# Down projections as seven block products in a hybrid encoder's FFN, on one Trainium2 core

## What is computed

```
for l in range(2):
  h = x + 0.5 * swiglu(rmsnorm(x, ffn1_norm), wg, wu, wd)
  p = rmsnorm(h) @ w_in ; retention heads and differential attention heads
  h = h + concat(ret, dif) @ w_out
  h = h + 0.5 * swiglu(rmsnorm(h, ffn2_norm), wg, wu, wd)
  x = rmsnorm(h, final_norm)
swiglu(x) = (silu(x @ wg) * (x @ wu)) @ wd
```

## Time and profile before

| | us |
|---|---|
| median of 3 runs (lowest, highest) | 1898.19 (1897.99, 1898.59) |
| the profiled execution | 1898.53 |
| its span | 1896.70 |
| PE busy | 1879.3 |
| POOL busy | 1206.0 |
| DVE busy | 1143.2 |
| ACT busy | 910.6 |

### The profile page before, as it was taken

One profiled execution on the slowest core, in us unless ns is written; L12 is line 12 of the kernel. 1 busy time (PEld: TensorE's weight loads), 2 busy tenths in 40 slices (PEclk: granted clock), 3 DMA queues, 4 the chain that ended last, 5 costly groups with the idle time before them and its releaser, 6 DMA issues.

```text
span 1896.7 us, 29712 instructions
## 1 busy us (share of the span) xinstructions
PE 1879.3 (99%) x11518; PEld 1673.4 (88%) x11518; DVE 1143.2 (60%) x1865; ACT 910.6 (48%) x1505; POOL 1206.0 (64%) x814
## 2 busy tenths in 40 slices
PE   9999999999999999999999999999999999999997
PEld 7989989878888989989889898998778889899896
DVE  7727657438756745727676476663587477366273
ACT  7525445456425534524565254445564365255252
POOL 6867767555435767857468576765554377678582
PEclk9999999999999999999999999999999999999999
DMA  4333323232223232332224223223222133324231
GB/s 157 137 99 125 134 84 112 78 100 67 67 67 111 90 112 90 106 97 105 83 101 157 73 106 112 89 90 111 78 67 78 46 111 112 111 90 134 67 110 69
DMA packets 54999, 186.46 MB, mean 98 GB/s; under 512 B 6440, under 2 KB 7976, under 8 KB 54860
## 3 DMA queue, kind: packets, MB, share of 16 engines
q1 hardware_dynamic: 53136, 181.61, 28.7%
q10 hardware_dynamic: 1724, 2.96, 0.5%
HBM read 182.44 MB, written 3.15 MB: 98 GB/s over the span
## 4 chain that ended last, share of the span: by engine, by line
PE 88%; POOL 6%; DVE 2%; ACT 2%; issue 1%; DMA 0%; SPq 0%; DVEq 0%; ACTq 0%; POOLq 0%
PE bank L693 17%; PE bank L695 17%; PE bank L694 17%; PE pair L693 9%; PE pair L695 9%; PE pair L694 9%; POOL w_lo L596 2%; PE pair L988 1%; POOL w_lo_x L615 1%; POOL w_lo L615 1%; PE pair L1012 1%; PE bank L973 1%; PE bank L1024 1%; PE bank L731 1%; PE bank L740 1%
## 5 line engine op out<-in xcount | busy, mean ns | idle before, releaser
L587 POOL TENSOR_TENSOR w_lo<-raw,w_hi 128x512 fp32r<-128x512 f32 (+1 forms) x240 | 314.8, 1336 | 382.5 <-ACT w_hi L1091 382.2
L693 PE MATMUL bank<-hg_hi,w_hi 128*128 128x256 f32 (+1 forms) x1396 | 447.1, 320 | 0.7 <-DVE bank L1581 0.7
L694 PE MATMUL bank<-hg_lo,w_hi 128*128 128x256 f32 (+1 forms) x1396 | 441.4, 316 | 0.0
L695 PE MATMUL bank<-hg_hi,w_lo 128*128 128x256 f32 (+1 forms) x1396 | 441.2, 316 | 0.0
L693 PEld LDWEIGHTS bank<-hg_hi,w_hi 128*128 128x128 f32 x1396 | 264.8, 190 | 22.1 <-issue 3.9
L694 PEld LDWEIGHTS bank<-hg_lo,w_hi 128*128 128x128 f32 x1396 | 265.0, 190 | 18.2 <-issue 1.2
L695 PEld LDWEIGHTS bank<-hg_hi,w_lo 128*128 128x128 f32 x1396 | 265.1, 190 | 17.6
L1091 ACT ACTIVATE w_hi<-raw 128x1024 fp32r<-128x1024 f32 (+1 forms) x120 | 124.2, 1035 | 262.2 <-PE bank L695 124.6
L1548 DVE SCALAR_TENSOR_TENSOR h<-pair,h 128x512 f32<-128x512 f32 x100 | 68.9, 690 | 258.6 <-PE pair L695 258.5
L693 PE MATMUL pair<-a_hi,w_hi 128*128 128x512 f32 x440 | 172.7, 393 | 1.9 <-issue 1.3
L695 PE MATMUL pair<-a_hi,w_lo 128*128 128x512 f32 x440 | 171.7, 390 | 0.0
(11 more groups left out here) (292 smaller groups left out, 4904.0 us busy)
## 6 DMA issues: line engine op xcount, KB each, us to landing
raw<-in_w_gu SPq DMA_DIRECT2D x96, 512.0 KB, 3.7
raw_x<-in_w_gu SPq DMA_DIRECT2D x80, 512.0 KB, 4.1
raw<-in_w_p SPq DMA_DIRECT2D x56, 512.0 KB, 3.5
raw_x<-in_w_dn SPq DMA_DIRECT2D x32, 512.0 KB, 3.8
raw<-in_w_dn SPq DMA_DIRECT2D x32, 512.0 KB, 3.6
raw<-in_w_o SPq DMA_DIRECT2D x16, 512.0 KB, 3.4
raw_x<-in_w_dn SPq DMA_DIRECT2D x16, 384.0 KB, 3.4
raw<-in_w_dn SPq DMA_DIRECT2D x16, 384.0 KB, 3.5
```

Source lines behind the costliest of these rows:

```text
L587: ins = pool.tensor_tensor(columns(lo_[:, part, :]), source[:, part.start * P:part.stop * P], columns(hi[:, part, :]).bitcast(F32), ALU.su ...
L693: pe.matmul(out, hi[:, 0, :], m_hi, start=first, stop=False)
L694: pe.matmul(out, hi[:, 0, :], m_lo, start=False, stop=False)
L695: return pe.matmul(out, lo_[:, 0, :], m_hi, start=False, stop=last)
```

## The change

The down projections of the first two chunks (PAIRED = 2) become blocks of the same kind as fast tiles. A block takes two output tiles (2q, 2q + 1) by even and odd gated tiles, tokens halved, so four blocks of 84 matmuls take the place of eight units. Blocks and tiles form one list of 28 per FFN, and all engines walk it in one order. The third chunk keeps its plain units. What a block needs of the activations is made for each pair of gated tiles: S1 to S4, sums and differences of token halves of the even and the odd tile.

```diff
+BLOCKS = []
+for _c in range(len(CHUNKS)):
+    BLOCKS += [("t", _c, _i) for _i in range(0 if _c else CLASSIC, CHUNKS[_c])]
+    if _c < PAIRED:
+        BLOCKS += [("d", _c, _q) for _q in range(KD // 2)]
...
+            def lo_s2(l, f, c, j):
+                n = mixture_index(f, c, j)
+                pool.wait_ge(s2_hi, at(s2_hi, l, n + 1))
+                pool.tensor_tensor(s2_l[:, j, :], even[:, 0:SEQ], s2_h[:, j, :].bitcast(F32), ALU.subtract)\
+                    .then_inc(s2_lo, 1)
```

POOL's queue in an FFN, after the classic units and the opening of the first two blocks, both as before:

```diff
+                for b in range(NB):
+                    kind, c, i = BLOCKS[b - 1] if b else ("", 0, 0)
+                    if kind == "t" and c < PAIRED and i % 2:
+                        lo_s2(l, f, c, i // 2)
+                    if b + 1 < NB:
+                        lo_differences(l, f, b + 1)
+                        lo_b22(l, f, b + 1)
+                    if b == 0:
+                        lo_s2(l, f, 0, 0)
+                    if b + 2 < NB:
+                        lo_gate(l, f, b + 2)
+                        differences(l, f, b + 2)
+                    elif b + 2 == NB:
+                        lo(l, down_unit(f, 0))
```

ACT's queue in the slot of block b (c and i are those of the block before it):

```diff
+                if kind == "t":
+                    silu(l, f, c, i)
+                copy_p1(l, f, b)
+                if not first_pair(b):
+                    hi_t4(l, f, b)
+                if paired and i % 2 == 0:
+                    copy_even(l, f, c, i)
+                if kind == "t":
+                    hi_gated(l, f, c, i)
+                if first_pair(b):
+                    hi_t4(l, f, b)
+                if paired and i % 2:
+                    hi_s14(l, f, c, i // 2)
+                    hi_s2(l, f, c, i // 2)
+                if b + 1 < NB:
+                    copy_t1(l, f, b + 1)
+                    hi_differences(l, f, b + 1)
+                    hi_t2(l, f, b + 1)
+                    hi_b22(l, f, b + 1)
```

DVE, with waits left out; for c < PAIRED fast_mult ends in gated_product, without the second product with the norm. FUNCTIONS_AT is {0: 1, 2: 2, 4: 3}. ACT makes its exponentials of part 0 before step 0 and those of part 2 after step 3's silu:

```diff
             def classic_up(l, f, i):
-                dve.tensor_tensor(up[:, :], gate_up[i][1], norm(f), ALU.mult).then_inc(up_ready, 1)
+                dve.tensor_copy(up[:, :], gate_up[i][1]).then_inc(up_ready, 1)
...
+            def gated_product(l, f, c, i):
+                if i % 2:
+                    dve.tensor_tensor(gated, gated, up[:, :], ALU.mult).then_inc(act_ready, 1)
+                    return
+                dve.tensor_tensor(gated[:, 0:SEQ], gated[:, 0:SEQ], up[:, 0:SEQ], ALU.mult)
+                dve.tensor_tensor(even[:, SEQ:T], gated[:, SEQ:T], up[:, SEQ:T], ALU.mult).then_inc(act_ready, 1)
+            def token_difference(l, f, c, i):
+                dve.tensor_tensor(gated[:, SEQ:T], gated[:, 0:SEQ], even[:, SEQ:T], ALU.subtract).then_inc(s3_done, 1)
+            def gated_mixtures(l, f, c, i):
...
+                dve.tensor_tensor(even[:, 0:SEQ], even[:, 0:SEQ], gated[:, SEQ:T], ALU.subtract).then_inc(s2_done, 1)
+                dve.tensor_tensor(s14[:, 0:SEQ], gated[:, SEQ:T], even[:, SEQ:T], ALU.add).then_inc(s1_done, 1)
+                dve.tensor_tensor(s14[:, SEQ:T], gated[:, 0:SEQ], even[:, 0:SEQ], ALU.add).then_inc(s4_done, 1)
+            def pair_outputs(l, f, b):
...
+                for out in (gated, odd_out):
+                    dve.scalar_tensor_tensor(out=out, in0=out, scalar=0.5, in1=norm(f), op0=ALU.mult, op1=ALU.mult)
+                for k, out in ((2 * q, gated), (2 * q + 1, odd_out)):
+                    dve.tensor_tensor(h[:, k, :], out, h[:, k, :], ALU.add).then_inc(h_ready, 1)
+            def former_output(l, f, b):
+                if l and f == 0 and 2 <= b < 2 + KD:
+                    scale_h(l - 1, b - 2)
...
             def attention(l):
+                layer_functions(l, 0)
                 dve.wait_ge(rms_ready, at(rms_ready, l, 2))
...
+                    if t in FUNCTIONS_AT:
+                        layer_functions(l, FUNCTIONS_AT[t])
```

More of the change, by code:

```diff
@@ L97 @@
     TILES_OF += [UT] * (2 * CLASSIC)
[L98 to L104, removed]
+    for _b in range(NB):
+        for _w in range(2):
+            RAW_AT["t", index(_f, _b), _w] = 2 * (1 - _b % 2) + _w
+    for _k in range(KD):
+        RAW_AT["e", down_unit(_f, _k)] = 2 * (1 - _k // 2 % 2) + _k % 2
+    TILES_OF += [CHUNKS[-1]] * KD
     if _f == 0:
@@ L342, in build @@
         up_ready = signal("up_ready", 2 * CLASSIC)
[L343 to L352, removed]
@@ L842, in classic_tiles, with fast_product @@
                     product(gate_up[1][s - 2], CLASSIC_SLOT[s], hg_hi, hg_lo, KD).then_inc(gu_done, 1)
-            def fast_product(q, w, half, m_hi, m_lo):
-                for k in range(KH):
-                    last = three(prod[q], (w, KH * half + k), m_hi[:, k, :], m_lo[:, k, :], k == 0, k == KH - 1)
-                last.then_inc(p_done[q], 1)
+            def fast_product(q, w, half, m_hi, m_lo, ks=range(KH), out=None):
+                for k in ks:
+                    last = three(prod[q] if out is None else out, (w, KH * half + k), m_hi[:, k, :], m_lo[:, k, :], k == 0, k == KH - 1)
+                if ks[-1] == KH - 1:
+                    last.then_inc(p_done[q], 1)
             def blocks_of(rows, half):
@@ L1128, in copy_t1, with hi_b22 @@
+            def hi_b22(l, f, b):
+                raw_wait(l, ("t", index(f, b), 1))
+                slot_free(l, f, b, 2, 3)
+                hi, _ = w_tiles(FAST_SLOTS[b % 2][2], KH, KH)
+                act.activation(columns(hi), raw_block(b, 1, 1), ACT.Copy).then_inc(b22_hi, 1)
+            def copy_t1(l, f, b):
+                m = index(f, b)
                 act.wait_ge(t13_done, at(t13_done, l, m + 1))
@@ L1380, in next_chunk @@
[L1380 to L1390 removed]
+                for b in range(NB):
+                    block_slot(l, f, b)
+                c, n = len(CHUNKS) - 1, CHUNKS[-1]
@@ new lines, in sum_t4, with lo_t @@
+            def sum_t4(l, f, b):
+                dve.wait_ge(x_lo, at(x_lo, l, 2 * index(f, b) + 1))
+                dve.tensor_tensor(t_sum, t_sum, raw_block(b, 0, 1), ALU.add).then_inc(t4_done, 1)
+            def lo_t(l, f, b, which):
+                dve.wait_ge(x_hi, at(x_hi, l, 2 * index(f, b) + which + 1))
+                hi, lo_ = w_tiles(t4_slot(b) if which else FAST_SLOTS[b % 2][2], KH)
+                dve.tensor_tensor(columns(lo_), t_sum, columns(hi).bitcast(F32), ALU.subtract).then_inc(x_lo, 1)
@@ L1675, in opening_tiles @@
                 if first:
[L1676 removed]
+                    sum_t2(l, f, 0)
                 mix_low(l, f, 2)
@@ new lines, in ffn @@
+                for b in range(NB):
+                    block_slot(l, f, b)
+                c, n = len(CHUNKS) - 1, CHUNKS[-1]
+                fast_gate(l, f, NB - 1)
+                fast_mult(l, f, NB - 1)
+                lo_gated(l, f, c, n - 1)
+                if f == 0:
+                    dve.wait_ge(par_in, at(par_in, l, 16 * 6))
+                for k in range(KD):
+                    add_output(l, down_output(f, k), k, down[k % 2], 0.5)
+                    if f == 0:
+                        lo_part(l, 1, k, par_at("mix_g", k))
+                        add_square(l, 0, k)
+                    else:
+                        if k < KD - 1:
+                            add_square(l, 2, k)
+                        if l == DEPTH - 1:
+                            continue
+                        lo_part(l, 3, k, next_gain[:, k:k + 1])
+                        add_next_square(l, KD, k, next_sq)
@@ L2014 @@
         for c, n in enumerate(CHUNKS):
-            w_dn[:, f, c, :, :, 0:n] = down[:, :, :, j:j + n]
+            ks = [*range(0, n, 2), *range(1, n, 2)] if c < PAIRED else [*range(n)]
+            w_dn[:, f, c, :, :, 0:n] = down[:, :, :, [j + k for k in ks]]
             j += n
```

797 lines of the change are left out of this document (441 added, 356 removed).

## The result

The changed kernel takes 1931.15 us (median of 4 runs, 1931.09 to 1931.22), the kernel before beside it 1898.28 (1897.99 to 1898.59): ratio 1.0171, 95% interval 1.0158 to 1.0184. It is slower by 32.9 us; the profiled span grew from 1896.7 to 1929.3, by 32.6.

A forecast was written before the change was run, and what follows sets the result against it. The prediction took a GpSimd-ScalarE loop of 10.53 us per block, against 10.0 of matmuls, to bound the kernel. Terms 17.7 + 4.6 + 2.7 + 1.5 + 2.9 = 29.4 on 1898.5 gave 1928, range 1912 to 1948.

The forecast's parts named there:

- The loop, +17.7: FFN blocks: GpSimd and ScalarE wait on each other, 26 cycles of 10.53 us; +4.4 per FFN, +17.7 for four.
- lo_s2 hidden but for the first: GpSimd's added subtraction fits its 1.69 us idle time, cost 0, except the first of each FFN, +0.65.
- rival B: After odd tiles, sums converted too late expose lo_s2 and copy_t1: +18 to +28 us, about 1950; chance 0.13.
- The opening, +0.5 per FFN for token_difference and copy_even: Start of each FFN: these two operations stand in a chain ending at the second block's L615, +0.5 us.
- scale_h, +2.7: Eight scalings in block slots of layer 1's first FFN take 0.33 us each of GpSimd's cycle; bounds 0 and 5.5.
- opening_pair, +1.5: First block of each down part: product 7 runs second, about 1 us stall; +1.5 over eight blocks, bounds 0 and 8.
- Attention, +2.9: Decay tables in attention's first steps delay a ScalarE conversion and the statistic behind it: 1.45 us per layer, bounds 0 and 4.
- hangs on it by the same distance: End of each FFN: six tiles of down projection follow the last block at the same distance as before.
- TensorE's busy time, -33 forecast: Whole kernel: TensorE's busy time falls by some 33 us while the span grows.

The follow-up runs named there:

- 53 us of matmuls less: Changed kernel without the third matmul (low part of the weights) of block product 3, part of the result left out: 1928.71 us.
- 0.52 less in the loop: Changed kernel with ScalarE's hi_differences ahead of copy_t1 in each block: 1892.34 us, 38.8 below the changed kernel.
- the same edit: Kernel before with ScalarE's hi_differences ahead of copy_t1: 1896.62 us, ratio 0.9988, 2.1 less.
- the spreading: Changed kernel with the four decay tables made one a step in attention steps 4 to 7, scaled in step 8: 1919.56 us.

## Why the prediction was right, and where it was not

1928 was forecast and 1931.15 came, inside the range and with the sign. The mechanism was the one that the cycle of GpSimd told; two terms were off, in opposite directions.

- **The loop, +17.7.** Its 26 cycles per FFN, without lo_s2 and scale_h, cost 23.5 - 2.8 - 3.5 = 17.2 (1.0 of it belongs to the three longer cycles below). Three runs bear it out: 53 us of matmuls less took only 1.2 us from the blocks, 0.52 less in the loop gave 48 us there, and the same edit gave 2 in the kernel before.
- **lo_s2 hidden but for the first.** The first cycle is 11.20 (45.11 to 56.31) instead of 10.52, +0.7 per FFN, +2.8 for four against 4 x 0.65. Its exposure after odd tiles, rival B, doesn't occur: 0.99 of idle time is left.
- **The opening, +0.5 per FFN for token_difference and copy_even.** The first two L658 of an FFN are 0.46 further apart than the first two L615 were in the first FFN and 0.42 in the third, the same in every run but for 0.01. In the second and fourth that distance goes from 9.9 to 12.0 from run to run, so there it can't be told.
- **scale_h, +2.7.** Measured 3.5, 0.44 each; the upper bound of 5.5 was too high.
- **opening_pair, +1.5.** TensorE waits 1.4 in each, as read ("about 1"), but the cycles there are 10.5 outside the third FFN, where one is 0.4 longer, with copy_t1 1.11 behind lo_t: 0.4 in all. Two further cycles are 0.3 longer, one in the third and one in the fourth FFN. In both GpSimd stands idle for 0.43 ahead of L650, and the transfer that L650 needs had landed 9 us before it in the third; the cause stays open. That copy_t1 was level at this spot was read rightly, and the run with lo_s2 on VectorE shows what one more operation costs.
- **Attention, +2.9.** This is the term that was mis-sized. What the spreading gives back is 11.6, 5.8 per layer where I had 1.45 and an upper bound of 4, and 0.67 and 1.2 are left. I had priced VectorE's part 2 at "at most 4 us", from its duration when it ran beside down units, and looked only at the statistic behind it. It took 7.6 (386.41 to 394.0), for four of its eight operations met GpSimd's; part 1 took 7.0. What was late was the step's next take-over and with it a PSUM bank (3.84 of wait), then the clock (1.4 and 2.5), and only at the end the statistic (1.12 and 0.30). The forecast followed the wrong wait.
- **What follows the last block "hangs on it by the same distance".** It did not. In the kernel before, last L615 and first matmul of the plain down units (timelines of GpSimd and TensorE); below them that matmul in the changed kernel, where the last L658 is at 319.10:

```profile
314.11 2.41 POOL L615 TENSOR_TENSOR w_lo_x<-raw,w_hi_x 128x1024 fp32r<-128x1024 f32 x1 [1.70 <-ACT w_hi_x L1117]
...
325.73 0.40 PE L693 MATMUL pair<-a_hi,w_hi 128*128 128x512 f32 x1
...
329.14 0.40 PE L737 MATMUL pair<-a_hi,w_hi 128*128 128x512 f32 x1
```

Before, TensorE ended an FFN 11.62 behind GpSimd and had work to catch up; now it keeps step, and the distance is 10.04. The other three FFNs show the same two distances within 0.04, so this gives four times 1.6, about -6. With fewer matmuls the distance is 9.57 and with the shorter loop 12.4, and the stretch to the next opening moves by -0.4 and +2.4 with it. This term and attention's, +9, cancelled in part, and that the sum came so close is luck to this extent: without this term the forecast would have been low by 9.
- **TensorE's busy time, -33 forecast.** It fell by 6.5. A 256-column matmul is shown 0.28 long while the next one starts 0.12 later, so every wait hides 0.16 of its length in the busy time: 73 waits in the rows above, 12 us. The two stretches at the lower clock are 4 more. Delays too short to be shown as idle time at all, counted from start to start, come to 5 to 9 us more than before (an estimate, since it hangs on where one draws the line to a usual distance). The few us that remain I can't place.

## What to carry to other kernels

When an engine at 64% busy has the same idle time in each cycle, ended by the same instruction, follow the loop through both engines and count its length against the work of the busiest engine; a phase that only seems to be slow work may be what gives that loop its lead. Shorten such a loop by the order of the instructions on the engine that releases it, after asking which buffer each moved instruction frees. Price a moved VectorE operation at its duration beside GpSimd, not where it stood alone, and ask which PSUM bank is taken over behind it. And compare where two engines stand at the end of a phase: how far the one lags behind the other is paid in the next.

## What was unexpected of the hardware

A VectorE operation on 128x8 takes 0.17 alone and 1.20 or 1.22 where GpSimd's 512-column operation, 1.27 each, runs beside it: it ends when that one ends. The tables' tensor_scalar of 384 columns goes from 0.41 to 1.45, with one tensor in SBUF as input. In the other direction GpSimd's L665 went from 1.31 to 1.75 when scale_h had started first. The Trainium skill, SBUF — State Buffer, section Who interferes with whom, says that a VectorE instruction with two SBUF inputs and a GpSimd instruction that reads SBUF shut each other out for the whole of the one that came first, and that tensor_scalar in a two-port mode does so with GpSimd too. The trace agrees in both directions, with 1.20 for 0.17 on VectorE and 0.44 more on GpSimd, which had 0.59 to wait until scale_h ended at 1020.65. The forecast cited that rule for scale_h and did not apply it to the tables, where it mattered more.
